# Row halves kept and fetched, weights split once: a two-layer hybrid transformer block on one Trainium2 core

## The reference

```python
for l in range(DEPTH):                                   # 2 layers
    hx = rmsnorm(x, norm_g[l]) * (1.0 + sc[:, None]) + sh[:, None]
    hc = rmsnorm(ctx, norm_g[l]) * (1.0 + sc_c) + sh_c
    px = split_cols(hx @ w_in[l])                        # all mixers and the gates read the same rows
    pcx = split_cols(hc @ w_in[l])
    a_l, a_c = diff_attention(px[0:3], pcx[0:3], ...)
    b_l, b_c = mlstm_mixer(px[3:8], pcx[3:8], ...)
    c_l, c_c = gla_mixer(px[8:12], pcx[8:12], ...)
    d_l, d_c = window_gqa(px[12:15], pcx[12:15], ...)
    y = jnp.concatenate([a_l, b_l, c_l, d_l], axis=-1) * jax.nn.silu(px[15])
    x = x + gt[:, None] * (y @ w_out[l])
```

## The kernel before

| projection | groups: tokens x columns |
|---|---|
| mLSTM (L498) | 640 x 272 twice, then 1280 x 256 twice |
| GLA (L1065) | 640 x 288 twice, then 512 and 768 tokens x 256 |
| differential (project_qk, L1452) | 640 x 512 twice (query, key), 640 x 256 twice (value) |
| windowed (project_qk) | 640 x 512 twice |

## Time and profile before

### The profile page before, as it was taken

The page is one execution under the profiler, slowest core; times in us unless marked ns, Lnnn a source line. Parts: engine busy times, 40 slices in busy tenths (PEclk is TensorE's granted clock), DMA queues, the critical chain, the costliest instruction groups (busy, mean ns, idle before and its releaser), DMA issues. The chain is left out here.

```text
span 2525.2 us, 38434 instructions
## 1 busy us (share of the span) xinstructions
PE 2032.9 (81%) x14664; PEld 1671.5 (66%) x14664; DVE 1715.3 (68%) x3007; ACT 1205.9 (48%) x2366; POOL 420.7 (17%) x404
## 2 busy tenths in 40 slices
PE   4879789776777677899978887987876776878988
PEld 2768668665556556787856766866665555667877
DVE  2576668688869477765745566687678785667656
ACT  4563352354868545533226543433447676445321
POOL 0003115132010020022220013044220000200222
PEclk7999899898989888999998988999978988979999
DMA  8200010000000100001333000000000001000121
GB/s 332 86 18 2 18 50 2 1 1 1 1 1 1 51 34 1 34 34 67 139 122 144 20 18 16 36 18 2 1 1 1 1 1 50 34 1 35 67 84 51
DMA packets 18502, 99.50 MB, mean 39 GB/s; under 512 B 2288, under 2 KB 2576, under 8 KB 13072
## 3 DMA queue, kind: packets, MB, share of 16 engines
q1 hardware_dynamic: 13136, 87.59, 9.1%
q10 hardware_dynamic: 5184, 9.44, 1.0%
HBM read 87.50 MB, written 9.44 MB: 38 GB/s over the span
## 5 line engine op out<-in xcount | busy, mean ns | idle before, releaser
L1964 DVE TENSOR_REDUCE a_st<-ps 128x1 f32<-128x1280 f32 (+1 forms) x144 | 196.7, 1368 | 44.6 <-PE ps L1849 44.0
L1917 ACT ACTIVATE ring<-ps,a_st 128x1280 f32<-128x1280 f32 (+1 forms) x144 | 177.4, 1232 | 56.2 <-DVE a_st L1964 56.0
L1849 PE MATMUL ps<-a_k,a_q 128*128 128x512 f32 (+1 forms) x400 | 128.1, 432 | 52.9 <-ACT ring L1917 48.5
L467 PE MATMUL ps<-a_proj_wh,a_proj_xh 128*128 128x512 f32 (+1 forms) x320 | 117.7, 368 | 52.1 <-DVE a_proj_xl L448 52.1
L2237 PE MATMUL ps<-g_x_hi,g_w_hi 128*128 128x512 f32 (+1 forms) x400 | 149.2, 373 | 9.7 <-DVE g_x_lo L2298 9.2
L2238 PE MATMUL ps<-g_x_lo,g_w_hi 128*128 128x512 f32 (+1 forms) x400 | 148.4, 371 | 0.0
L2239 PE MATMUL ps<-g_x_hi,g_w_lo 128*128 128x512 f32 (+1 forms) x400 | 148.2, 370 | 0.0
L2261 ACT ACTIVATE g_x_hi<-hT 128x512 fp32r<-128x512 f32 (+1 forms) x120 | 70.3, 589 | 159.7 <-PE ps L2239 152.9
L2298 DVE TENSOR_TENSOR g_x_lo<-hT,g_x_hi 128x512 fp32r<-128x512 f32 (+1 forms) x120 | 84.6, 710 | 86.5 <-ACT g_x_hi L2261 85.6
L1866 PE MATMUL ps<-cst,ring 128*128 128x128 f32 x656 | 105.5, 293 | 42.5 <-ACT ring L1926 16.9
L1849 PEld LDWEIGHTS ps<-a_k,a_q 128*128 128x128 f32 x400 | 74.7, 215 | 82.8 <-ACT ring L1917 66.0
(11 more groups left out here) (398 smaller groups left out, 6190.6 us busy)
## 6 DMA issues: line engine op xcount, KB each, us to landing
ring<-in_w SPq DMA_DIRECT2D x22, 2048.0 KB, 7.5
yT<-in_w SPq DMA_DIRECT2D x4, 2048.0 KB, 9.6
latents<-hT ACTq DMA_DIRECT2D x32, 256.0 KB, 2.0
ring<-in_w SPq DMA_DIRECT2D x6, 1024.0 KB, 5.5
hT<-in_tok SPq DMA_DIRECT2D x10, 512.0 KB, 15.2
hT<-in_tok SPq DMA_DIRECT2D x20, 256.0 KB, 5.9
hT<-latents SPq DMA_DIRECT2D x16, 256.0 KB, 6.0
cst<-in_cst SPq DMA_DIRECT2D x1, 2763.0 KB, 14.6
```

The lines of the kernel that those rows point to most:

```text
L467: last = pe.matmul(out, left, right, start=k == 0 and j == 0, stop=k == KT - 1 and j == 2)
L1849: last = pe.matmul(ps[:, 3 * c + b, 0:w], q4[:, 2 * h + c, t * P:(t + 1) * P], k4[:, 2 * h + c, k0:k0 + w], start=True, stop=True)
L1917: act.activation(p(u, c, n), ps[:, 3 * c:3 * c + 3, :].rearrange("p b n -> p (b n)")[:, 0:n], ACT.Exp, bias=st[:, 0:1], accum_out=st[:, 1: ...
L1964: dve.tensor_reduce(stat[:, u % SLOTS, c, 0:1], ps[:, 3 * c:3 * c + 3, :].rearrange("p b n -> p (b n)")[:, 0:n], AX.X, ALU.max, negate=Tru ...
```

## The change

The rows are split once per layer, in the norm stage. ScalarE now evicts all 24 jobs into a four-slot buffer, POOL casts each to the high part, which takes hT's memory (h_hi is a view of it in fp32r), VectorE subtracts, and SyncE stores the low part to DRAM (h_low). Every projection reads the resident high part, and fetches the low part of each step from DRAM by a transfer that POOL issues, through three buffers: fetch i waits until step i - 3 has been multiplied. In POOL's queue these fetches now stand among its other work, at steps written out by hand.

The weights of a slab are split once for all its groups ("sets"): ScalarE makes the high part up to four steps ahead, VectorE writes the low part over the slab itself (ring_lo). SyncE gives the slab free once its last group is multiplied (release). In the gates, ScalarE and VectorE lose the row splits. In the GLA, TensorE waits for the new signal first_decays ahead of eight filler products (WARM), and for one more eviction ahead of the logits of tiles 2 and 3.

Numbers of steps and so of fetches in the run: 32 in each mLSTM, GLA and differential projection, 16 in each windowed one, 72 in the gates of layer 0 and 48 in those of layer 1, 344 in all. There are 48 casts, 48 subtractions and 48 stores in the two norm stages.

```diff
@@ stage_norm
+        h = own.enter_context(env["sbuf"]("h_whole", [P, SLOTS, BANK], F32))
+        lo = own.enter_context(env["sbuf"]("h_low", [P, KT, T], F32R))
...
+        @block.scalar
+        def _(act):
+            for n, (k, (v, t0, m)) in enumerate(jobs):
+                act.wait_ge(turned.sem, n + 1)
+                if n >= SLOTS:
+                    act.wait_ge(low.sem, n - SLOTS + 1)
+                act.activation(h[:, n % SLOTS, 0:m * P], ps[:, n % 4, 0:m * P], ACT.Identity,
+                               bias=mod_cols[:, 0, k, v:v + 1], scale=mod_cols[:, 1, k, v:v + 1]).then_inc(kept.sem, 1)
+
+        @block.gpsimd
+        def _(pool):
+            for n, (k, (v, t0, m)) in enumerate(jobs):
+                pool.wait_ge(kept.sem, n + 1)
+                pool.tensor_copy(h_high(n), h[:, n % SLOTS, 0:m * P]).then_inc(high.sem, 1)
+
+        @block.vector
+        def _(dve):
+            for n, (k, (v, t0, m)) in enumerate(jobs):
+                dve.wait_ge(high.sem, n + 1)
+                dve.tensor_tensor(lo[:, k, toks(n)], h[:, n % SLOTS, 0:m * P], h_high(n).bitcast(F32), ALU.subtract).then_inc(low.sem, 1)
+
+        @block.sync
+        def _(sp):
+            for n, (k, _) in enumerate(jobs):
+                sp.wait_ge(low.sem, n + 1)
+                sp.dma_start(low_part(env, k, toks(n)), lo[:, k, toks(n)].bitcast(F32)).then_inc(stored.sem, 16)
+            sp.wait_ge(stored.sem, 16 * len(jobs))
...
@@ LowParts
+    def fetch(self, pool, i):
+
+        k, t0, m = self.steps[i]
+        pool.dma_start(self.x[:, i % self.bufs, 0:m], low_part(self.env, k, slice(t0, t0 + m)))\
+            .then_inc(self.env["fetched"][i % self.bufs].sem, 16)
...
@@ SplitProduct
+    AHEAD = 4
...
+        self.sets = [g for g, q in enumerate(groups) if g == 0 or groups[g - 1][0:3] != q[0:3]]
...
+    def due(self, i):
+
+        ahead = range(min(self.AHEAD, len(self.steps))) if i == 0 else ()
+        return [self.steps[n] for n in (*ahead, i + self.AHEAD) if n < len(self.steps) and self.steps[n][0] in self.sets]
...
     def high(self, act, i):
+        for g, k in self.due(i):
+            self.wait_slab(act, g, k)
+            if g > 0:
+                self.wait_used(act, KT * (g - 1) + k)
+            act.activation(self.w_hi[:, k, 0:self.groups[g][2]], self.weight(g, k), ACT.Copy).then_inc(self.w_high.sem, 1)
+
+    def low(self, dve, i):
+
+        for g, k in self.due(i):
+            self.wait_slab(dve, g, k)
+            w = self.weight(g, k)
+            dve.wait_ge(self.w_high.sem, KT * self.set_of(g) + k + 1)
+            dve.tensor_tensor(self.weight(g, k, "ring_lo"), w, self.w_hi[:, k, 0:self.groups[g][2]].bitcast(F32), ALU.subtract)\
+               .then_inc(self.weights.sem, 1)
+
+    def fetch(self, pool, i):
+
+        if i >= self.x_lo.bufs:
+            self.wait_used(pool, i - self.x_lo.bufs)
+        self.x_lo.fetch(pool, i)
+
+    def release(self, engine, g):
+
+        engine.wait_ge(self.ready.sem, self.first[g + 1])
+        engine.sem_inc(self.env["slab_used"].sem, 1)
...
@@ SplitProduct.multiply
-        pe.wait_ge(self.hi.sem, i + 1)
-        pe.wait_ge(self.weights.sem, i + 1)
-        pe.wait_ge(self.lo.sem, i + 1)
+        pe.wait_ge(self.weights.sem, KT * self.set_of(g) + k + 1)
+        x_lo = self.x_lo.wait(pe, i)
...
+            w = [self.w_hi[:, k, cols], w_lo[:, cols]]
+            x = [self.env["h_hi"][:, k, t0 + toks.start:t0 + toks.stop], x_lo[:, toks]]
...
@@ stage_mlstm, gpsimd
+                for i, (g, k) in enumerate(proj.steps):
+                    proj.fetch(pool, i)
+                    if (g, k) == (2, 2):
+                        pool.wait_ge(mod_mm.sem, 2)
+                        pool.wait_ge(v_ones.sem, 2)
+                        pool.memset(yT[:, 0, :], 0.0).then_inc(v_ones.sem, 1)
...
@@ stage_gla
+                pe.wait_ge(first_decays.sem, 1)
                 for _ in range(WARM):
...
@@ project_qk, gpsimd
+            after = {(g, k): t for t, (g, k) in enumerate([(1, 4), (1, 5), (1, 6), (1, 7), (2, 0)] if halves else [(1, 4), (1, 5), (1, 6), (1, 7)])}
+            if halves:
+                after.update({(g, k): HN + a for a, (g, k) in enumerate([(2, 4), (2, 5), (2, 6), (2, 7), (3, 0)])})
+            for i, (g, k) in enumerate(proj.steps):
+                proj.fetch(pool, i)
+                if (g, k) in after:
+                    gain(after[g, k])
...
@@ stage_gates, gpsimd
+            for i, (g, k) in enumerate(steps):
+                if i >= low.bufs:
+                    pool.wait_ge(step_mm.sem, i - low.bufs + 1)
+                low.fetch(pool, i)
+                if g >= 1 and 3 <= k < 3 + groups[g - 1][2]:
+                    gated(first[g - 1] + k - 3)
```

More of the change, by code:

```diff
@@ L402, in __init__ @@
         toks, cols = max(q[4] for q in groups), max(q[2] for q in groups)
-        part = lambda n, width: own.enter_context(env["sbuf"](f"{name}_{n}", [P, self.BUFS, width], F32R))
-        self.x_hi, self.x_lo = part("xh", toks), part("xl", toks)
-        self.w_hi, self.w_lo = part("wh", cols), part("wl", cols)
+        self.x_lo = LowParts(env, own, f"{name}_xl", [(k, *groups[g][3:5]) for g, k in self.steps], toks)
+        self.w_hi = own.enter_context(env["sbuf"](f"{name}_wh", [P, KT, cols], F32R))
@@ new lines, in set_of, with weight, wait_slab @@
+    def set_of(self, g):
+        return max(i for i, at in enumerate(self.sets) if at <= g)
+    def weight(self, g, k, of="ring"):
+        s, c0, w = self.groups[g][0:3]
+        return slab(self.env, s, of)[:, k, c0:c0 + w]
+    def due(self, i):
+        ahead = range(min(self.AHEAD, len(self.steps))) if i == 0 else ()
+        return [self.steps[n] for n in (*ahead, i + self.AHEAD) if n < len(self.steps) and self.steps[n][0] in self.sets]
+    def wait_slab(self, engine, g, k):
+        s = self.groups[g][0]
+        if k == 0 and (g == 0 or self.groups[g - 1][0] != s):
+            engine.wait_ge(self.env["loaded"][s].sem, 16)
@@ L1111, in _ @@
                 pool.memset(lrT[2 * RANK:2 * RANK + 1, :], 1.0).then_inc(ones_set.sem, 1)
+                for i in range(len(proj.steps)):
+                    proj.fetch(pool, i)
                 pool.wait_ge(ones_set.sem, 1)
@@ L1595, in _, with gain @@
         def _(pool):
-            for t in range(NT):
+            def gain(t):
                 x = raw[:, t % HN, :]
@@ L2213, in stage_gates @@
     with ExitStack() as own, nc.Block() as block:
-        x_hi, x_lo = (own.enter_context(env["sbuf"](f"g_x_{n}", [P, BUFS, BANK], F32R)) for n in ("hi", "lo"))
+        low = LowParts(env, own, "g_x_lo", [(k, *groups[g][3]) for g, k in steps], BANK)
         w_hi, w_lo = (own.enter_context(env["sbuf"](f"g_w_{n}", [P, KT, BANK], F32R)) for n in ("hi", "lo"))
@@ L2306, in _, with gated @@
         def _(pool):
-            for n, (g, c) in enumerate(sums):
+            def gated(n):
+                g, c = sums[n]
                 s, y0, m, b = groups[g]
@@ L2313, in _ @@
                     pool.wait_ge(done.sem, n + 1)
+            for i, (g, k) in enumerate(steps):
[4 more added lines that the diff above has]
+                    gated(first[g - 1] + k - 3)
+            for n in range(first[-2], first[-1]):
+                gated(n)
             pool.wait_ge(done.sem, len(sums))
```

185 lines of the change are left out of this document (81 added, 104 removed).

## The result

| | before | changed |
|---|---|---|
| median | 2529.55 us (2524.63 to 2532.84, 4 runs) | 2584.88 us (2580.55 to 2594.51, 4 runs) |
| ratio | | 1.0212, 95% interval 1.018 to 1.0244 |
| span of the profiled execution | 2525.2 us | 2580.5 us |
| VectorE, ScalarE busy | 1715.3, 1205.9 us | 1403.2, 969.3 us |
| POOL busy | 420.7 us | 631.6 us |

A forecast was written before the change was run, and what follows sets the result against it. TensorE sets the time where the splits keep up, VectorE's two subtractions a step where they do not. Terms sum to -8.6 in layer 0 and -16.1 in layer 1, together -24.7 against 2527.95 us: 2503, range 2465 to 2585.

The forecast's parts named there:

- The fetch's price, L = 3.4 us: Time from POOL's issue to the landing of 640 tokens (320 KB): line through two SyncE transfers, 2.7 us, plus 0.7.
- Each fetch takes L: In all projections and gates, every fetch of 320 KB was priced at 3.4 us, other sizes scaled alike.
- the floor: Per projection, the number of steps times TensorE's least time for a step; 83.2 us in the differential projection.
- Starts, +6.9 a layer: Five stage starts: the first product waits for a fetch to land, 18.6 us a layer instead of 11.75.
- The norm stage, +15.7: Norm stage, each layer: 26.3 us instead of 10.6, with 1.1 or 0.6 us a job, filling and the last store.
- mLSTM -15.5, windowed -6.5, differential -8: Change per layer, in us, in these three projections from removing the row splits and the weights' second splitting.
- GLA -9.2: GLA projection, each layer: 10.5 us taken back, less 1.3 for the third group's 256 KB fetches.
- Gates +8.0 and +0.5: Gates of layers 0 and 1, us: back to least step times, plus late fetches and, in layer 0, POOL's multiplies.
- (L+S)/3: With three buffers, a step takes the larger of this and S, TensorE's least time for the step.
- Rival "round trip too long": The slower rival: fetch round trips bound steps; no gain from L about 3.85, 2557 at 4.3, 2601 at 5.0; chance 0.33.
- The signs that I gave: Slower: gate steps at 1.7 us or more with TensorE waiting for DMA, or first products over 4 us after a barrier.

The follow-up runs named there:

- fifth run: The changed kernel with every fetch issued by SyncE instead of POOL, into the same three buffers; 2513.03 us, ratio 0.9918 to the kernel before.
- third run: The changed kernel with six buffers instead of three for the low rows in the gates; 2558.55 us, ratio 1.0109 to the kernel before.
- the sixth: The changed kernel with slab loads of the third mLSTM and GLA groups issued after the projection's last step; 2576.25 us, ratio 1.0163.
- the ninth: The changed kernel with SyncE issuing fetches, six gate buffers, modulation and GLA loads in pieces, mLSTM and GLA slab loads deferred; 2462.63 us, ratio 0.9742.
- eleventh run: The changed kernel with the norm stage's cast to the high part on VectorE instead of POOL; 2584.00 us, ratio 1.0221.
- first run: The changed kernel with only the first three fetches of each projection and of the gates, later steps rereading those buffers; 2473.89 us, ratio 0.9768.
- fourth run: The kernel before with weights split once, only in the two attentions, rows split every step through two buffers; 2565.39 us, ratio 1.0134.

## Why the prediction was wrong, point by point

- **The fetch's price, L = 3.4 us:** right to 0.2 us for a fetch that is alone, 3.2 by the trace. The line through the two rows of SyncE's gives 2.8, 2.6, 2.2 and 3.8 us for 320, 256, 128 and 640 KB, a little above what I wrote; the fifth run, with SyncE as issuer, measured 2.9, 2.6, 2.0 and 3.9. What I added for POOL, 0.7, was 0.3. My reason for it was also misread: the earlier trace rows has a POOL instruction of 0.17 us, and a fetch occupied POOL for 0.53. The rule of the Trainium skill, "DMA: Bandwidth & Descriptors" (Anatomy of one DMA), comes to 2.75 us for 320 KB by its fit, worked out as an estimate, and was 0.45 low against the median of 3.2.
- **"Each fetch takes L":** this is the step that failed. I took L from rows of transfers that were alone, and gave it to every fetch, also to those that SyncE's weight loads stand beside. I had even written of these loads only that they come later and cost nothing. The trace of before held the warning: its transfers of 1024 KB take 5.0 us, and the slab loads, which are issued inside projections, more:

```profile
ring<-in_w SPq DMA_DIRECT2D x22, 2048.0 KB, 7.5
```

  By the runs, it cost some 18 and 14 us in the gates (the groups with a slab load, third run), 7 a layer in the GLA's third group (the sixth) and 7 to 8 a layer at the start of the mLSTM (the ninth). That is some 60 us of the 80 by which the kernel missed the forecast. POOL's own queue, which the fifth run shows to be as dear, was for the most part in the sum: in the differential projection I had left 23.9 us over the floor, and 23.4 were there. Its drains were not (below).
- **Starts, +6.9 a layer:** 17.3 by the trace of layer 0. The first products came 11.2, 6.3, 3.9, 4.0 and 3.5 us after their barriers, the first two behind loads.
- **The norm stage, +15.7:** +13.2. It took 25.3 us where I had 26.3, but I had set this against 10.6 us, the time to the end of TensorE's work, where the stage took 12.1 up to the barrier. The period of a job was 1.02 us where I had 1.1, and the last store and the way out of the barrier took 3.0 us from VectorE's last subtraction. The eleventh run shows that the two engines together do a job hardly faster than VectorE alone (1.02 us against 1.06). The Trainium skill's rule in "SBUF — State Buffer" (Who interferes with whom) agrees in direction, with the 1.07 us of the subtraction here against 0.69 alone and the cast's 1.01 against 0.61, but not in size: the 1.30 us a job of full exclusion were never reached.
- **mLSTM -15.5, windowed -6.5, differential -8:** -14.3, -4.8 and -8.5, right; the third mLSTM group took 29.1 us, as I had said. In the differential one it is in part luck, since the parts were others than I wrote: its second group fell to 28.0 us, its floor, and the value half took 48.9 us where its floor is 28.4, held up by POOL's queue.
- **GLA -9.2:** +1.5, by the load (7) and the first steps; without the load, in the sixth run, it took 70.2 us against my 68.0.
- **Gates +8.0 and +0.5:** +28.9 and +17.6, as above. The pace of (L+S)/3 was right for fetches alone: the fewest steps in the 512-token groups of the small slab were 1.36 to 1.55 us, against 1.52.
- **Not in the sum at all:** at the end of the gates 6.8 and 4.8 us pass between POOL's last multiply and the next stage's first instruction, 0.9 in the kernel before. That is +5.9 and +3.9.
- **Rival "round trip too long":** it gave the sign and a size (2557 at L = 4.3), but by a mechanism that was not the one at work; L was 3.2. The top of my range, 2585, stood for L about 4.75 in every fetch, so that the kernel came out there is luck. Its sentence that nothing but POOL's promptness helps was wrong: six buffers helped.
- **The signs that I gave:** those of the slower rival came, first products 11.2 and 6.3 us after a barrier and gate steps of 1.7 us and more with TensorE waiting for the DMA, but from loads and from POOL's order, at L = 3.2. I had given no sign that would have told a long round trip from a fetch beside a load.

For layer 0 the parts sum to 13.2+17.3-14.3+1.5-8.5-4.8+28.9+5.9 = +39 us; the trace has +32 from the norm stage's start to the output stage. The difference lies in stretches that were not edited: 4 between the GLA's and the differential projection, most of it in the scan, where the granted clock was 0.94 instead of 0.89, and 3 in the attention behind the differential projection (259.9 us instead of 262.4, clock 0.91 instead of 0.88). Why the clock moved, no run settles.

## What to carry to other kernels

Before work is moved from an engine to small transfers, list every large load that the queues issue in the same stretch, and give the transfers that fall beside one the large load's time, not their own. Keep such loads out of the way: defer them to where nothing is fetched, or cut them into small pieces between fetches (here the pieces' DMA packets became small as well, and which of the two did it is not shown); a load moved in one piece to where fetches still run only moves the wait. And issue fetches from a queue that holds nothing else that waits, with enough buffers to bridge the longest transfer that they can meet.

## What the runs showed of the hardware that I had not expected

- A fetch issued while a large load is in flight lands about when the load does, not in its turn by size: fetches of 320 KB issued 0.5 to 1.8 us after 4 MB of loads took 10.2 to 13.4 us, the first of them landing between the two loads, the others within 1.2 us behind the second. With both in SyncE's queue (the fifth run) they took 12.2 to 13.3 us. The Trainium skill, "DMA: Bandwidth & Descriptors" (Queues, rings and completion order), has each DMA engine take turns, packet by packet, between the queues that have work. If the turns were of equal bytes, a fetch in POOL's queue would lose about its own transfer time to the load, some 1.1 us by the step from 320 to 640 KB (3.2 to 4.3 us), and land after 4.3 us, an estimate. The packets that the trace records say what the turns were instead. At the start of the mLSTM, between 81.1 and 88.9 us, 172 packets of 2560 bytes (POOL's fetches) and 173 of 16384 bytes (SyncE's loads) started: as many of one queue as of the other, so the load moved more than six bytes for each of the fetch's. In the gates it was 35 packets of 2048 bytes against 38 of 16384. These counts agree with turns by packets; a packet was one partition's row of the transfer, and the load's rows are long.
- Ahead of these turns stands a wait: beside a load, a fetch's first packet started 3.0 to 4.5 us after the issue (8 cases), alone after 1.2 (the median of 92). In the fifth run, with both in one queue, there were no turns: the fetches' first packet started at 88.98 us, when the loads' last was starting (89.27).
- POOL's queue has a cost at the end of a stage that grew with the number of transfers it had issued. The trace records an instruction DRAIN of POOL's there:

```
gates, layer 0, 72 fetches    1216.18  5.93 us   POOL L2308 DRAIN
gates, layer 1, 48 fetches    2475.41  3.97 us   POOL L2308 DRAIN
windowed, 16 fetches           934.52  1.35 us   POOL L1553 DRAIN
first run's gates, 3 fetches  1178.36  0.29 us   POOL L2311 DRAIN
```

  That is 82 to 97 ns a fetch, where the last fetch had long landed. Where 31 or 32 fetches stood ahead and the last was still in flight (mLSTM, GLA and differential projection), the DRAIN took 5.3, 4.6 and 4.6 us and ended 1.4 us after that fetch had landed. Where other engines still work it is hidden; at the end of the gates it is not.
- A POOL-issued fetch occupied POOL for 0.53 us and landed 0.3 us later than the same one of SyncE's (3.2 against 2.9 us for 320 KB).
- In the differential projection the steady step of 15 products went from 3.40 to 3.50 us with the weights' low part read from the ring; the fourth run, which has only the single weight split, has 3.48. No run tells why.
